# A two-block layer kernel on one core: w_out, down projection and w_o stream the high and low activation halves as one 512-column matmul

## The reference, cut to what matters

```python
# block 1
h = rmsnorm(x, norm_mix);  p = h @ w_in                      # 2048 x 4352
y_a, y_b, y_c = pool_mixer(p), hyena_mixer(p), gating(p)
x = x + concat(y_a, y_b, y_c) @ w_out                        # 2048 x 2048
h = rmsnorm(x, norm_ffn)
up = dwconv3(h @ ffn_w_up);  gate, val = split(up)           # 2048 x 11264
x = x + (silu(gate) * val) @ ffn_w_down                      # 5632 x 2048
x = rmsnorm(x, norm_final)
# block 2
h = rms_norm(x, norm_g);  proj = h @ w_in_2
ya, yb, yc = band_attention(...), rwkv7(...), memory_attention(...)
merged = sig(ga) * (ya @ w_up_a) + sig(gb) * (yb @ w_up_b) + sig(gc) * (yc @ w_up_c)
return x + merged @ w_o                                      # 2048 x 2048
```

## Time and profile before

| | |
|---|---|
| Median of 3 runs | 2539.17 us (2537.14 to 2540.28) |
| Span of the profiled execution | 2537.8 us |
| TensorE busy, matmuls | 2455.0 us, 19960 matmuls |
| DVE busy | 1534.1 us |
| ACT busy | 1185.9 us |
| Mean granted TensorE clock | 0.985 |
| w_out, from 292.8 us | 256 triples, 90.5 us |
| down projection, from 652.4 and 1035.0 us | 704 triples, 2 x 124.4 us |
| w_o, from 2444.0 us | 256 triples, 90.5 us |

### The profile page before, as it was taken

The page is one execution under the profiler, slowest core; times in us unless marked ns, Lnnn a source line. Parts: engine busy times, 40 slices in busy tenths (PEclk is TensorE's granted clock), DMA queues, the critical chain, the costliest instruction groups (busy, mean ns, idle before and its releaser), DMA issues.

```text
span 2537.8 us, 51128 instructions
## 1 busy us (share of the span) xinstructions
PE 2455.0 (97%) x19960; PEld 2413.6 (95%) x19960; DVE 1534.1 (60%) x2050; ACT 1185.9 (47%) x1502; POOL 12.8 (1%) x27
## 2 busy tenths in 40 slices
PE   6999998999999999997899999999999999999999
PEld 6898997999999999996899999999999999999999
DVE  6456566666555666566866666766576454544454
ACT  5343335665434666434444445444465443434433
POOL 0000000000000000000000000000000000000000
PEclk9999898999999999998999999999999999999999
DMA  6353354555554555554333333333355355555554
GB/s 233 130 180 116 129 187 132 188 170 194 183 186 167 183 181 189 179 185 147 117 119 112 109 120 111 119 123 104 118 175 173 125 184 179 185 176 175 184 187 160
DMA packets 110145, 400.39 MB, mean 158 GB/s; under 512 B 12394, under 2 KB 12421, under 8 KB 109904
## 3 DMA queue, kind: packets, MB, share of 16 engines
q1 hardware_dynamic: 108000, 391.00, 46.4%
q0 software_dynamic: 2032, 7.67, 0.9%
HBM read 396.52 MB, written 2.10 MB: 157 GB/s over the span
## 4 chain that ended last, share of the span: by engine, by line
PE 92%; DVE 5%; issue 1%; ACT 1%; DMA 0%; DVEq 0%; SPq 0%; ACTq 0%
PE bank L417 91%; DVE w_lo L1316 1%; ACT w_hi L909 1%; DVE scratch L1365 1%; PE bank L611 0%; DVE s_k L1365 0%; DVE h_lo L1362 0%; DMA x<-in_xT 0%; DVE cum L1362 0%; DVE root L1404 0%; DVE ping L1362 0%; DVE s_t L1362 0%; DVE qr L1807 0%; DVE acc L1362 0%; DVE s_t L1369 0%
## 5 line engine op out<-in xcount | busy, mean ns | idle before, releaser
L1316 DVE TENSOR_TENSOR w_lo<-raw,w_hi 128x1024 fp32r<-128x1024 f32 x736 | 892.0, 1224 | 803.8 <-ACT w_hi L909 797.5
L909 ACT ACTIVATE w_hi<-raw 128x1024 fp32r<-128x1024 f32 x736 | 770.7, 1057 | 1018.7 <-PE bank L417 999.5
L417 PE MATMUL bank<-h_hi,w_hi 128*128 128x256 f32 x4016 | 1163.3, 290 | 36.6 <-DVE h_lo L1362 15.0
L417 PE MATMUL bank<-h_lo,w_hi 128*128 128x256 f32 x4016 | 1141.0, 284 | 0.0
L417 PE MATMUL bank<-h_hi,w_lo 128*128 128x256 f32 x4016 | 1140.8, 284 | 0.0
L417 PEld LDWEIGHTS bank<-h_hi,w_hi 128*128 128x128 f32 x4016 | 775.6, 193 | 47.0 <-issue 24.4
L417 PEld LDWEIGHTS bank<-h_lo,w_hi 128*128 128x128 f32 x4016 | 775.9, 193 | 3.3 <-issue 2.2
L417 PEld LDWEIGHTS bank<-h_hi,w_lo 128*128 128x128 f32 x4016 | 775.0, 193 | 0.0
L417 PE MATMUL bank<-m_hi,w_lo 128*128 128x256 f32 x704 | 197.8, 281 | 0.0
L417 PE MATMUL bank<-m_hi,w_hi 128*128 128x256 f32 x704 | 197.1, 280 | 0.0
L417 PE MATMUL bank<-m_lo,w_hi 128*128 128x256 f32 x704 | 195.7, 278 | 0.0
(11 more groups left out here) (414 smaller groups left out, 2820.2 us busy)
## 6 DMA issues: line engine op xcount, KB each, us to landing
raw<-in_units SPq DMA_DIRECT2D x736, 512.0 KB, 3.4
x<-in_xT SPq DMA_DIRECT2D x4, 512.0 KB, 5.8
memx<-in_memT POOLq DMA_DIRECT2D x4, 512.0 KB, 7.2
out_y<-obuf SPq DMA_DIRECT2D x8, 256.0 KB, 4.3
bias_t<-in_bias POOLq DMA_DIRECT2D x8, 192.0 KB, 2.9
dft<-in_dft POOLq DMA_DIRECT2D x1, 1024.0 KB, 7.6
decay<-in_decay POOLq DMA_DIRECT2D x1, 768.0 KB, 5.6
con<-in_con SPq DMA_DIRECT2D x1, 546.0 KB, 7.8
```

The costliest lines, as they stand in the source:

```text
L417: return pe.matmul(out, lhsT, rhs, start=start, stop=stop, skip_group_check=True)
L909: return act.activation(out, in_, ACT.Copy, scale=scale)
L1316: dve.tensor_tensor(w_lo[slot][:, :, :], raw[slot][:, :, :], w_hi[slot][:, :, :].bitcast(F32), ALU.subtract).then_inc(split_done, 1)
```

## The change

- All eight PSUM banks are taken as four tensors of two banks (`wide`), and each pair of activation tiles becomes one tensor of two halves (`h_both`, `y_both`, `m_both`, `mg_both`), with the old names as views of it. For h, y and m the two halves lie where they lay. `mg_both` starts at offset 0 of the arena, and ya, gate, macc, mtmp and obuf move up by 8 KB.
- In w_out, down projection and w_o, w_hi is loaded once for one matmul of 512 columns over `both[:, :, k, :]` (256 high columns, then 256 low ones, from two places). Its results fill a bank: the high product in columns 0 to 255 and the low one in 256 to 511. The matmul of w_lo adds into columns 0 to 255. An output tile has a bank to itself, a group of two tiles has two banks.
- The residual addition becomes two: x plus columns 0 to 255 of both banks, then plus columns 256 to 511 of both, 128 x 512 each. The second waits for the first and carries the `bank_read` count. In the down projection the order is: first addition of both pairs, a wait, second addition of both pairs.
- TensorE waits for `bank_read` of bank 0 and of bank 1 ahead of the w_out loop and ahead of the w_o loop, since the wide pairs cover banks which the narrow groups used under the other number. The up projection uses the first bank of wide pairs 0 and 1.

The diff, cut to its core:

```diff
+        wide = [ctx.enter_context(nc.psum_tensor(f"wide{i}", [P, 2, 2 * T], F32)) for i in range(4)]
+        banks = [wide[i // 2][:, i % 2, :] for i in range(8)]
...
+        y_both = place("y_both", [P, 2, KT, T], 0, F32R)
+        y_hi, y_lo = y_both[:, 0], y_both[:, 1]
...
+        UP = [wide[0][:, 0, :], wide[1][:, 0, :]]
+        WIDE = [wide[0], wide[1], wide[2], wide[3]]
+
+        def part_of(b, s):
+            return WIDE[b][:, :, s * T:(s + 1) * T]
...
+            def wide_unit(bank, k0, both, first, last):
+
+                slot = next(slots) % RING
+                pe.wait_ge(split_done, n.next("split"))
+                for kk in range(UK):
+                    for t in range(2):
+                        o = WIDE[bank][:, t, :]
+                        mm(o, w_hi[slot][:, kk, t * P:(t + 1) * P], both[:, :, k0 + kk, :], first and kk == 0, False)
+                        m = mm(o[:, 0:T], w_lo[slot][:, kk, t * P:(t + 1) * P], both[:, 0, k0 + kk, :], False,
+                               last and kk == UK - 1)
+                m.then_inc(unit_used, 1)
...
+            for b in (0, 1):
+                pe.wait_ge(bank_read[b], n.now(("fill", b)))
             with n.loop(4, {("fill", 0): 1, ("fill", 1): 1, "split": 8}):
-                group(1, y_hi, y_lo, ready=(dve_for_pe, (most, most, most, rest)))
-                group(0, y_hi, y_lo)
+                wide_group(1, y_both, ready=(dve_for_pe, (most, most, most, rest)))
+                wide_group(0, y_both)
...
-                                o = p2(pair[t // 2])[:, t % 2, :]
+                                o = WIDE[pair[t // 2]][:, t % 2, :]
...
-                                mm(o, wh, rh, u == 0 and kk == 0 and t % 2 == 0, False)
-                                mm(o, wh, rl, False, False)
-                                m = mm(o, wl, rh, False, u == 10 and kk == 1 and t % 2 == 1)
+                                mm(o, wh, m_both[:, :, 2 * u + kk, :], u == 0 and kk == 0, False)
+                                m = mm(o[:, 0:T], wl, m_both[:, 0, 2 * u + kk, :], False, u == 10 and kk == 1)
...
+            for b in (0, 1):
+                pe.wait_ge(bank_read[b], n.now(("fill", b)))
             with n.loop(4, {("fill", 0): 1, ("fill", 1): 1, "split": 8}):
-                group(0, mg_hi, mg_lo, ready=(merged_ready, (6, 6, 6, 8)))
-                group(1, mg_hi, mg_lo)
+                wide_group(0, mg_both, ready=(merged_ready, (6, 6, 6, 8)))
+                wide_group(1, mg_both)
...
-                read(tt(dst, t, p2(b), ALU.add), b)
+                step(tt(dst, t, part_of(b, 0), ALU.add))
+                settle()
+                read(tt(dst, dst, part_of(b, 1), ALU.add), b)
```

More of the change, by code:

```diff
@@ L417, in mm, with unit @@
                 return pe.matmul(out, lhsT, rhs, start=start, stop=stop, skip_group_check=True)
-            def unit(bank, k0, hi, lo, first, last, tiles=2, fresh=True):
+            def unit(bank, k0, hi, lo, first, last, tiles=2, of=None):
                 slot = next(slots) % RING
                 pe.wait_ge(split_done, n.next("split"))
-                o = p2(bank)
+                o = p2(bank, of)
                 for kk in range(UK):
@@ L432, in unit, with wide_group, group @@
                 m.then_inc(unit_used, 1)
-            def group(bank, hi, lo, k0=0, units=4, tiles=2, filled=True, arriving=False, ready=None):
+            def wide_unit(bank, k0, both, first, last):
[8 more added lines that the diff above has]
+                m.then_inc(unit_used, 1)
+            def wide_group(bank, both, units=4, ready=None):
+                pe.wait_ge(bank_read[bank], n.now(("fill", bank)))
+                n.next(("fill", bank))
+                for u in range(units):
+                    if ready:
+                        pe.wait_ge(ready[0], ready[1][u])
+                    wide_unit(bank, UK * u, both, u == 0, u == units - 1)
+            def group(bank, hi, lo, k0=0, units=4, tiles=2, filled=True, arriving=False, ready=None, of=None):
                 if filled:
@@ L445, in group @@
                         pe.wait_ge(ready[0], ready[1][u])
-                    unit(bank, k0 + UK * u, hi, lo, u == 0, u == units - 1, tiles)
+                    unit(bank, k0 + UK * u, hi, lo, u == 0, u == units - 1, tiles, of)
             def from_dve(k=1):
@@ L572, in _ @@
                     for b in (1, 0):
-                        group(b, h_hi, h_lo, ready=(dve_for_pe, quarters) if b else None)
+                        group(b, h_hi, h_lo, ready=(dve_for_pe, quarters) if b else None, of=UP)
                 for q in range(4):
@@ L1445, in hyena @@
                 n.next(("fill", b))
-                last = taps([dst[:, j + s, :] for s in range(2)], b, [col("hy_w", 2 * p + s) for s in range(2)],
+                last = taps([dst[:, j + s, :] for s in range(2)], p2(b), [col("hy_w", 2 * p + s) for s in range(2)],
                             [col("hy_w", 36 + 2 * p + s) for s in range(2)])
@@ L1614, in _ @@
                     par[:, COL["norm_g"]:COL["norm_g"] + KT], ALU.mult))
-            with n.loop(4, {"unit": 8, ("fill", 0): 1, ("fill", 1): 1, "step": 4}) as i:
+            with n.loop(4, {"unit": 8, ("fill", 0): 1, ("fill", 1): 1, "step": 6}) as i:
                 for q, b in enumerate((1, 0)):
@@ L1627, in _ @@
                 own_bank(b)
[L1628 removed]
+            with n.loop(2, {"unit": U_UP + U_DOWN, "act": 3 * FF_HALF, "to_act": 2 * FF_HALF, "step": 2 * FF_HALF + 39,
                             ("fill", 0): 13, ("fill", 1): 13, ("fill", 2): 2, ("fill", 3): 2}) as half:
@@ L1652, in _ @@
                     for s, b in enumerate((1, 0) if q % 2 else (2, 3)):
+                        t = x[:, 4 * q + 2 * s:4 * q + 2 * s + 2, :]
+                        step(tt(t, t, part_of(b, 0), ALU.add))
+                    settle()
+                    for s, b in enumerate((1, 0) if q % 2 else (2, 3)):
                         n.next(("fill", b))
                         t = x[:, 4 * q + 2 * s:4 * q + 2 * s + 2, :]
-                        read(tt(t, t, p2(b), ALU.add), b)
+                        read(tt(t, t, part_of(b, 1), ALU.add), b)
                     for s, b in enumerate((1, 0) if q % 2 else (2, 3)):
@@ L2008, in _ @@
                     dve.wait_ge(merged_ready, n.next("merged"))
-            with n.loop(3, {"unit": 8, ("fill", 0): 1, ("fill", 1): 1}) as i:
+            with n.loop(3, {"unit": 8, ("fill", 0): 1, ("fill", 1): 1, "step": 2}) as i:
                 for b in (0, 1):
```

44 lines of the change are left out of this document (20 added, 24 removed).

## The result

The kernel after the change takes 2548.17 us as the median of five runs (2547.73 to 2551.46); the kernel before took 2539.17 us in the same set (five runs, 2536.89 to 2540.68). The ratio is 1.0040, with a 95% interval of 1.0028 to 1.0051. The forecast was 2527.0 us, with a range up to 2539; the time lies outside it, on the other side of no change, and 2.1 us from the rival that was called "The excess is not the load's" (2546.1 us).

The account below looks back on a forecast made before the run. TensorE's matmuls, 97% of the span, were taken as the bound. Terms -23.1 + 2.0 + 3.3 + 1.6 + 0.7 + 1.3 + 1.3 + 0.7 = -12.2 us on 2537.8, plus 1.4 for the median: 2527.0 us, range 2516 to 2539.

Parts of the forecast that it names:

- The excess is not the load's: Rival: excess goes with the columns, wide matmul 230 ns or more, saving only 4.0 us; 2546.1 us, slower; chance 0.13.
- Part 1, the pair: In w_out, down projection and w_o, each triple of 353.4 ns becomes a pair of 334.4 ns; 23.1 us less.
- B: Second matmul of each pair, 256 columns with w_lo; claimed to stay at 117.8 ns.
- A: First matmul of each pair, 512 columns with w_hi; claimed 216.6 ns, 213.3 streaming plus 3.3.
- one small fixed share: Lower bound of the wide matmuls' gain: only 3.3 ns goes with the third instruction; 4.0 us saved.
- A keeps the whole 11.1 once: Lower bound of the wide matmuls' gain: A 224.4 ns, pair 342.2 ns; 13.6 us saved.
- Parts 2 and 3, the waits: TensorE waits for bank readers: ahead of w_out for Gelu, +2.0 us; ahead of w_o for the mtmp multiplication, +3.3 us.
- Part 4, the second addition: Exposed at ends of w_out +0.7, first down half +1.3, second down half +1.3 and kernel +0.7 us; elsewhere hidden.
- the tight step: Between two down projection groups: DVE's first split done at 9.9 us, due at 10.7; fits by 0.8 us.
- The clock: After the gap ahead of w_o, 3.2 us at half clock, half of it lost: +1.6 us.
- Transfers and moved tiles: Supply at 196 GB/s against 190, and mg moved from 78 to 0 KB: both priced at nothing.
- Each matmul keeps its 11.1 ns: Rival: A costs 224.4 ns, so -13.6 + 10.9 = -2.7 us; 2536.5 us; chance 0.13.

Follow-up runs that it names:

- experiment 1: No kernel computation, only series of 48 equal matmuls, 64 to 512 columns, three data types; fp32r took 227 ns at 512 columns, 120.0 at 256.
- e2_narrow: Changed kernel with each wide matmul undone into two narrow ones, banks, waits and two additions kept; 2550.77 us, ratio 1.0047.
- Experiment 2: Changed kernel with high and low activation halves side by side per tile, so a wide matmul reads one block; 2546.29 us, ratio 1.0026.
- experiment 5: No kernel computation, only fp32r matmul series at nine activation places, two weight places, three weight widths; 120.0 ns at all places, 227 with 512 columns.
- e3_nowait: Changed kernel without the waits ahead of w_out and w_o, which start in free banks; 2538.35 us, ratio 0.9995.
- e6_own_banks: Kernel without the two waits, plus last groups narrow with one addition, last down groups in own banks without a wait; 2534.24 us, ratio 0.9977.

## Why the prediction was wrong, step by step

**Part 1, the pair: the step that failed.** The term was 23.1 us and the trace gives 8.1. B was right (118.3 ns against 117.8). A was put at 216.6 ns and takes 228.4. It was made of 213.3 ns of streaming and 3.3 ns that came from a plain float32 matmul of 512 columns, on the ground that the 11 ns are a weight load looking out from under a short streaming. Two inferences carried this, and both were wrong. First, "exactly 213 ns at the lower clock, so the excess is hidden there": the floor of short fp32r matmuls, read as the load's period, rises from 111.7 to 213 ns with the clock (experiment 1), and such a row can't tell whether it is the load. Second, "A lies nearest to the row of 512 columns": it is near in columns, not in type. Series of one type put 13.3 ns on each fp32r matmul whatever its length from 256 to 512 columns (16 at 448), and 2.5 ns on each bf16 matmul and on each float32 row of two passes. A hint lay in the kernel before: "353.4 ns everywhere" holds for the changed stages, but the narrow matmuls on h, more than half of all, stood 120.0 ns apart there already. The term's true size lies between its two lower bounds, "one small fixed share" (4.0 us) and "A keeps the whole 11.1 once" (13.6). Note that merging two matmuls still should have saved one excess of 11.1 ns by this; it saved 6.7, since A has 15.1 over its 213.3 ns and not 11.1. What the fp32r excess is, is open. It isn't a fixed number of cycles, since at half clock A has none; and why the narrow matmuls in these stages have 11.1 ns (10.0 in w_out and w_o of e2_narrow) and those on h and in the series 13.3 isn't known.

**Parts 2 and 3, the waits.** Right in place and cause, near in size: w_out starts 2.2 us late (forecast 2.0) and w_o 3.7 us (3.3). The releasers are the Gelu's reading and the multiplication into mtmp, as read from the earlier trace rows.

**Part 4, the second addition.** Right: 0.7, 1.3, 1.3 and 0.7 us at the four ends, each within 0.03 us. The groups inside the down projection took it without an idle moment on TensorE, so the tight step did fit.

**The clock.** Forecast +1.6 us at w_o alone, measured 4.3 us in w_out and w_o, and a further 0.6 behind the gap between the halves, where 6.8 us stood at half clock and not 3.4. The step that failed is reading a bound off a few gaps: 2.36 us idle left the clock alone, so 2.07 us ahead of w_out was given no price, and it did drop the clock for 3.4 us. Experiment 2 shows the other side, 3.48 us idle and no drop. An idle time alone doesn't say what happens.

**Transfers and moved tiles** were rightly put at nothing: the window inside the down projection shows 190 GB/s, as before, and a tile's place doesn't matter (experiment 5).

**The rivals.** "The excess is not the load's" came within 2.1 us of the time, and had been given 0.13 on the strength of the two inferences above. That nearness is luck. Its mechanism, an excess that goes with the columns, is not what the series show. It priced the gain at 4.0 us against 10.9 of waits and clock; measured are 8.1 of gain, 9.9 of waits and additions and 6.0 of clock and unchanged stages, so its parts were off both ways. "Each matmul keeps its 11.1 ns" is nearer to the series, where each has the same excess, but it made A 224.4 ns and the kernel 2536.5 us. The prediction did name the mark, A over 226 ns. That the waits, and not the matmuls, decide the sign is shown by e3_nowait: with the same wide matmuls and no wait it is level with before.

## What to carry to other kernels

Price an instruction by a row of its own data type: at full clock one matmul has some 13 ns on top of its columns in fp32r and 2.5 ns in bf16, and merging two of fp32r gave back 6.7 ns here. When a small gain is spread over many instructions (6.7 ns, 1216 times), any wait that comes with it must be priced with the half clock that may follow, up to 2.7 us here; give the stage a bank that is free, and don't let a counter of readings ask for more than the bank that is used. Compare stage lengths between traces, not totals: with and without the wide form the changed stages differed by 5.3 us in one pair of kernels and by 7.3 in another, while the totals differed by 2.6 and by 20.8. And when an edit moves the code ahead of a long loop, look at the gaps behind its turns.

## What the runs showed of the chip that was not expected

- fp32r matmuls in a row have 13.3 ns each on top of columns / 2.4, from 256 to 512 columns (16 at 448), and never come closer than 111.7 ns; at half clock there is no excess with 256 or 512 columns.
- The same narrow triples keep 350.0 or 353.3 ns for a whole stage, with the same instructions and at full clock.
- The least distance of fp32r matmuls with 64 columns is 111.7 ns at full clock and 213 ns at half.
- The clock fell after 2.07 us of idle time in one place, and stayed up after 3.48 us in another; in the series it fell with no idle time. The same code had 3.4 us at half clock in one kernel and 6.8 in another.
- Four of TensorE's 41 branches take 4.3 to 4.4 us each in e6_own_banks, with a 16 KB instruction transfer inside; where a second transfer was awaited too, TensorE stood still for another 3 us, in a loop that the edit didn't touch.
- With a bf16 matmul in each triple of fp32r ones the triple takes 363 ns in place of 360: nothing is gained by mixing.
